# Loading each big weight chunk ahead of the small chunks around it, in the up parts of an expert layer

## The reference, cut to what matters

```python
def _swiglu(h, w_up, w_down):
    g, u = jnp.split(h @ w_up, 2, axis=-1)
    return (jax.nn.silu(g) * u) @ w_down

def _moe(h, w_router, w_up, w_down):
    ...
    top_val, top_idx = lax.top_k(logits, TOP_K)          # 2 of 8 experts for each token
    ...
    for e in range(N_EXPERTS):
        out = out + gates[:, e:e + 1] * _swiglu(hf, w_up[e], w_down[e])
```

## Time and profile before

| what | value |
|---|---|
| three runs | 1743.07, 1746.58, 1746.68 us |
| profiled execution, its time | 1743.41 us |
| its span, first to last instruction | 1741.3 us |
| TensorE busy (PE) | 1638.6 us, 94% |
| VectorE busy (DVE) | 873.3 us, 50% |
| ScalarE busy (ACT) | 652.4 us, 37% |
| moved by DMA | 481.98 MB, mean 277 GB/s |
| loads of expert chunks | 336 of 1 MB: 2 items of 168 |

### The profile page before, as it was taken

How to read it: one execution, slowest core, us unless ns; L and a number is a source line. 1 busy time by engine, 2 the same in 40 slices (tenths; PEclk the granted TensorE clock), 3 DMA queues, 4 the chain that set the end, 5 groups by cost and what they waited for, 6 DMA issues and landing times.

```text
span 1741.3 us, 28335 instructions
## 1 busy us (share of the span) xinstructions
PE 1638.6 (94%) x11532; PEld 1218.1 (70%) x11532; DVE 873.3 (50%) x1305; ACT 652.4 (37%) x956; POOL 28.7 (2%) x49
## 2 busy tenths in 40 slices
PE   5999999999999999999999999998998999899897
PEld 3886568899999777876766667765556666665564
DVE  2434764899997355743763233333433322323447
ACT  2324663544444333424733233333332322323232
POOL 1200000000000000000010000000000000000000
PEclk8999999999999999999999999999999999999999
DMA  9824863133334545333289999999999999999996
GB/s 349 197 97 171 322 233 97 49 98 98 98 122 157 206 146 172 118 97 121 98 297 408 421 421 410 390 401 416 415 422 420 421 421 420 419 416 417 417 417 257
DMA packets 117440, 481.98 MB, mean 277 GB/s; under 512 B 8218, under 2 KB 52424, under 8 KB 68928
## 3 DMA queue, kind: packets, MB, share of 16 engines
q1 hardware_dynamic: 114720, 472.66, 69.2%
q0 software_dynamic: 2592, 7.51, 2.0%
HBM read 477.27 MB, written 2.87 MB: 276 GB/s over the span
## 4 chain that ended last, share of the span: by engine, by line
PE 68%; DMA 13%; DVE 9%; ACT 5%; issue 5%; SPq 0%; DVEq 0%; ACTq 0%
PE PS L1020 17%; PE PS L1022 16%; PE PS L1021 16%; DMA RAWB<-in_w_exp_up 6%; PE PS L1680 4%; DMA RAWB<-in_w_exp_down 3%; PE PS L1052 3%; ACT BH L2346 2%; PE PS L1752 2%; PE PS L1309 2%; DMA RAWA<-in_w_exp_up 2%; DMA RAWA<-in_w_exp_down 1%; PE PS L1319 1%; PE PS L1331 1%; DVE RAWBL L3277 1%
## 5 line engine op out<-in xcount | busy, mean ns | idle before, releaser
L3277 DVE TENSOR_TENSOR RAWBL<-RAWB,BH 128x2048 fp32r<-128x2048 f32 x45 | 103.1, 2292 | 277.2 <-ACT BH L2346 277.2
L1020 PE MATMUL PS<-HH,WH 128*128 128x256 f32 (+1 forms) x600 | 193.5, 323 | 6.3 <-DVE HL L2577 2.9
L1020 PE MATMUL PS<-BH,HE 128*128 128x512 f32 x448 | 182.1, 406 | 12.6 <-DVE RAWBL L3277 11.8
L1022 PE MATMUL PS<-HH,WL 128*128 128x256 f32 (+1 forms) x600 | 190.6, 318 | 0.0
L1021 PE MATMUL PS<-HL,WH 128*128 128x256 f32 (+1 forms) x600 | 190.6, 318 | 0.0
L3277 DVE TENSOR_TENSOR RAWAL<-RAWA,BH 128x2048 fp32r<-128x2048 f32 x39 | 89.4, 2292 | 197.0 <-ACT BH L2346 196.4
L2346 ACT ACTIVATE BH<-RAWB 128x2048 fp32r<-128x2048 f32 x45 | 86.2, 1915 | 239.9 <-DMA RAWB<-in_w_exp_up 120.0
L1022 PE MATMUL PS<-BH,LE 128*128 128x512 f32 x448 | 175.9, 393 | 0.0
L2538 DVE TENSOR_TENSOR WL<-RAW,WH 128x2048 fp32r<-128x2048 f32 (+1 forms) x41 | 91.7, 2237 | 143.0 <-ACT WH L1950 142.7
L2346 ACT ACTIVATE BH<-RAWA 128x2048 fp32r<-128x2048 f32 x39 | 74.6, 1914 | 204.1 <-DMA RAWA<-in_w_exp_up 129.9
L1950 ACT ACTIVATE WH<-RAW 128x2048 fp32r<-128x2048 f32 (+1 forms) x41 | 76.8, 1874 | 141.4 <-PE PS L1022 141.3
(11 more groups left out here) (398 smaller groups left out, 3147.3 us busy)
## 6 DMA issues: line engine op xcount, KB each, us to landing
RAWB<-in_w_exp_up SPq DMA_DIRECT2D x106, 1024.0 KB, 10.5
RAWA<-in_w_exp_up SPq DMA_DIRECT2D x106, 1024.0 KB, 10.6
RAWA<-in_w_exp_down SPq DMA_DIRECT2D x56, 1024.0 KB, 10.0
RAWB<-in_w_exp_down SPq DMA_DIRECT2D x56, 1024.0 KB, 9.8
RAW<-in_w_mod SPq DMA_DIRECT2D x48, 1024.0 KB, 6.8
RAW<-in_w_ffn_up SPq DMA_DIRECT2D x22, 1024.0 KB, 5.5
RAW<-in_w_in_c SPq DMA_DIRECT2D x12, 1024.0 KB, 5.1
RAW<-in_w_ffn_down SPq DMA_DIRECT2D x10, 1024.0 KB, 7.2
```

Source lines behind the costliest of these rows:

```text
L1020: mm(ps, ah, bh, start=start, stop=False)
L1022: return mm(ps, al, bh, start=False, stop=stop)
L3277: v.tensor_tensor(expert_low(big_place(a, i), i), expert_raw(big_place(a, i), i), BH[:, a % 2, :].bitcast(F32), ALU.subtract).then_inc(s_b ...
```

## The change

The list of loads is changed in two places: `up_order`, from which all seven stages of a later item are made, and the last three stages of the first item in `order1`. In a stage of the loop the big chunks stand at places 0, 4, 8 and 12 in place of 2, 6, 10 and 14; in a stage of 12 of the first item they stand at 0, 2, 4 and 8 in place of 1, 3, 6 and 10. With the names from above a stage of the loop is loaded as B s s s B s s s B s s s B s s s, and a stage of 12 as B0 a0 B1 a1 B2 a2 a3 b0 B3 b1 b2 b3. The smalls keep their order among themselves, and so do the bigs.

```diff
-        up_order = [(0, 0), (0, 1), ("big", 0), (0, 2), (0, 3), (1, 0), ("big", 1), (1, 1),
...
+        up_order = [("big", 0), (0, 0), (0, 1), (0, 2), ("big", 1), (0, 3), (1, 0), (1, 1),
...
-            order1 += [(j0, "u", st0, 0), ("big", "u", st, 0), (j0, "u", st0, 1), ("big", "u", st, 1),
...
+            order1 += [("big", "u", st, 0), (j0, "u", st0, 0), ("big", "u", st, 1), (j0, "u", st0, 1),
...
```

More of the change, by code:

```diff
@@ L217, in trunk @@
         NST = EFT // 4
-        up_order = [(0, 0), (0, 1), ("big", 0), (0, 2), (0, 3), (1, 0), ("big", 1), (1, 1),
-                    (1, 2), (1, 3), ("big", 2), (2, 0), (2, 1), (2, 2), ("big", 3), (2, 3)]
+        up_order = [("big", 0), (0, 0), (0, 1), (0, 2), ("big", 1), (0, 3), (1, 0), (1, 1),
+                    ("big", 2), (1, 2), (1, 3), (2, 0), ("big", 3), (2, 1), (2, 2), (2, 3)]
         UPI = NS * NST
@@ L242, in trunk @@
             st = 4 + n
-            order1 += [(j0, "u", st0, 0), ("big", "u", st, 0), (j0, "u", st0, 1), ("big", "u", st, 1),
-                       (j0, "u", st0, 2), (j0, "u", st0, 3), ("big", "u", st, 2), (j1, "u", st1, 0), (j1, "u", st1, 1),
-                       (j1, "u", st1, 2), ("big", "u", st, 3), (j1, "u", st1, 3)]
+            order1 += [("big", "u", st, 0), (j0, "u", st0, 0), ("big", "u", st, 1), (j0, "u", st0, 1),
+                       ("big", "u", st, 2), (j0, "u", st0, 2), (j0, "u", st0, 3), (j1, "u", st1, 0),
+                       ("big", "u", st, 3), (j1, "u", st1, 1), (j1, "u", st1, 2), (j1, "u", st1, 3)]
         assert 1 + 3 * THREES == 4 * 4 and len(PAIRS) - THREES == NST - 4
```

## The result

| | before | after |
|---|---|---|
| runs, median (lowest to highest) | 20 runs: 1745.72 us (1741.98 to 1747.66) | 20 runs: 1749.32 us (1746.71 to 1751.48) |
| ratio | | 1.0027, 95% interval 1.0021 to 1.0033 |
| profiled execution, its span | 1743.41, 1741.3 us | 1749.56, 1747.4 us |

The change makes the kernel slower: by 0.27% or about 4.7 us by the ratio, while the medians lie 3.6 us apart and the means 4.1. The whole interval of the ratio lies just above the 0.2% that the prediction took for the least difference a measurement tells. Of the two profiled executions the one of after is 6.15 us longer. The twenty times of before fall into two groups, 1741.98 to 1745.12 and 1746.33 to 1747.66 us, and the profiled one belongs to the lower, so not all of the 6.15 us is the change's.

A forecast was written before the change was run, and what follows sets the result against it. The prediction took TensorE to bound the kernel from 1040 to 1170 us and the DMA engines afterwards until 1717 us. It added 2.3 us of first-item lag to 1746.58, giving 1748.9 us; 8-in-10 range 1743.5 to 1755.

The forecast's parts named there:

- The first item loses DMA time while TensorE is full: First item, places 76 to 111: waits for big chunks move forward and loads lose 8.7 us, against 5.9 before.
- The lag: 3.0 us at place 114, and at 118 1.5: First two big chunks of the first item's down part: they land 3.0 and 1.5 us later than before.
- the longer step: Between places 114 and 118 before: four chunks took 11.5 us, not 9.9; if repeated, the lag is 3.0, else 1.5.
- I take 2.3: First item's lag at the down part, taken between 1.5 and 3.0 us: 2.3 us added to the time.
- Landing of 5.55 us in a dry queue: First item: a load that finds the DMA queue nearly dry lands 5.55 us after issue; other cases took 7.0 and 7.7.
- In all 8.7 us lost, against 5.9 before: First item: losses of 2.5, 2.5, 1.9 and 1.8 us at places 86, 88, 100 and 112.
- 0.9 us of cover at places 88 and 100: First item: these big chunks are converted 0.9 us or more before TensorE comes to them.
- the upper bound: First item with dry landings of 7.7 us: TensorE 1.2 us late at places 88 and 100, +6 us in all.
- The second item's queue keeps full: Second item's up part: slot reloads have 7.4 or 7.0 us where 5.5 do, so this part costs nothing.
- the rival's mechanism: Second item: reloads leave after the big product and come too late, queue runs dry; 11 us more, 1760, chance 0.13.
- the rival that put 15.3 us on them: TensorE's waits for converted chunks from 1300 to 1600 us were the cost; removing them gives 1731.3 us, chance 0.07.
- The first stall of the second item shrinks: Second item's start: first big product starts about 1308.1, not 1311.4 us; clock may fall less, nothing gained in time.

The follow-up runs named there:

- first_only: Kernel before with the new load order only in the first item's last three stages and the second item's last up stage: 1749.72 us, ratio 1.0036.
- second_only: Kernel before with the new load order only in stages 0 to 5 of the second item: 1745.36 us, ratio 1.0010.
- second_by3: Kernel before with big chunks of the second item's stages 0 to 5 loaded three places earlier: 1764.41 us, ratio 1.0117.
- second_by4: Kernel before with big chunks of the second item's stages 0 to 5 loaded four places earlier: 1901.06 us, ratio 1.0904.
- light_after: Changed kernel with one product in place of three for big chunks in the first item's stages 4 to 6: 1741.10 us, 0.9985 of the kernel before.

## Why the prediction was right in kind and short in size

- *The first item loses DMA time while TensorE is full.* Right, and the loads of 86, 88, 100 and 112 left when B1 and B2 ended, as named; only 88 landed in a dry queue. `first_only` has the cost, and in `second_only` it is within the measurement.
- *The lag: 3.0 us at place 114, and at 118 1.5, or 3.0 if the longer step between landings comes again.* Counted from load 82 the pair of profiles shows 3.0 at 114, 1.5 at 118, and 3.0 from 122 on: the longer step came again, four chunks later.
- *"I take 2.3."* This is the step that failed. It averaged the two, as if the longer step were of that one execution. It should have taken 3.0 at least, and the profiles put 2.9 to 4.2 on the first item (`first_only` and after, loads 75 to 167), the runs 4.7 us by the ratio (3.7 to 5.8 us by its interval). That a landing computed without such steps was set against a recorded one with them made the forecast too small. The time of 1749.32 lies near the forecast of 1748.9 partly by luck: the median of three runs it was added to, 1746.58, is 0.9 above that of twenty. And with 2.3 in the sum the larger chance, 0.58, went to a time that counts as the same; slower, with 0.35, was right.
- *Landing of 5.55 us in a dry queue.* Measured 4.9, 4.8, 7.2 and 4.9. The three rows that it came from say little of a dry queue: each of these loads had 3.0 us of earlier loads still ahead when it left, and the one that took 5.5 us landed 2.5 us behind the load before it, without a gap. The 4.4 us, an estimate from the Trainium skill ("DMA: Bandwidth & Descriptors", Anatomy of one DMA) would have been nearer in three of four cases; the lags worked out from it, 1.9 us at 114 and 0.3 at 118, would have been farther off all the same.
- *In all 8.7 us lost, against 5.9 before.* From load 84 to 114 the landings lose 8.7 and 5.7 us against steps of 2.48, but otherwise spread, so the agreement is partly luck. Of the 2.5, 2.5, 1.9 and 1.8 us put on places 86, 88, 100 and 112, the landings show 0.7, 2.5, 2.8 and none; another 1.3 us are lost at 89, behind the dry queue, and 0.9 at 113.
- *TensorE not late before 1170 us, with 0.9 us of cover at places 88 and 100.* Right at 88; at 100, where the load took 7.2 us, the cover went, as the upper bound had it, and TensorE was later by 0.8 us at the next named issue. The trace after names 0.5 us of it as a wait for the converted chunk, the only one from 1040 to 1170 us:

```profile
PEld PS L1020 <- DVE RAWBL L3277: 0.5, 1, 0.5
```

- *The second item's queue keeps full.* Right: 419 GB/s. It has 27 batches behind a big product, and in the profile all of them left with 4.8 to 5.9 us of loads still to land, without a gap at their own landing. `second_by3` shows the rival's mechanism to be real, one place further on.
- *The waits for converted chunks go, without gain.* Right, against the rival that put 15.3 us on them. From 1300 to 1600 us no wait of L1020 for RAWBL or RAWAL is left among the larger ones; TensorE waits for small chunks in their place:

```profile
PEld PS L1680 <- DMA RAWB<-in_w_exp_up: 19.7, 12, 1.9
...
PE PS L1680 <- DMA RAWB<-in_w_exp_up: 15.4, 13, 1.5
```

- *The first stall of the second item shrinks, and the clock with it.* Right: 6.96 us busy for 2.28 and a granted clock of 1.00 for 0.75, worth nothing in the time. The first copy came at 1308.04 and not about 1304, since the loads were 5.9 us late by then.
- *391 to 394 GB/s from 1040 to 1170 us.* Too high: 383. 17 GB/s over 130 us are 5.3 us of loads, of which some 1.4 arise ahead of the change: the lag is 0.7 us at load 66, which lands as the stretch begins, and 2.1 at load 82.
- *The copy of the down part's first big chunk at 1168 to 1170 us.* It came at 1171.25; of its lag of 5.2 us, 2.1 were there before the change.

## What to carry to other kernels

Where one queue issues loads in order, and each waits for its slot, list them in the order in which the consumer frees the slots: a load moved ahead of that order takes its wait along, and every free slot behind it stands idle. Loading a slowly prepared tile "earlier" in such a ring should pay only if something waits for it on the path that sets the end (argued; no run with the full work gained by it). Here one to two places cost 1 to 2 chunks of transfer where the consumer is the bound, two places nothing clear of noise where the DMA engines are, and three places 15 to 18 us in either part. Compute both sides of a difference with the same model: a smooth replay of the new order against a recorded one of the old hides the steps that the replay leaves out.

## What the runs showed of the hardware

- A 1 MB load of the ring that found no load ahead of it landed 4.7 to 5.0 us after its issue (22 batches in `second_by4`, 4.8 at place 88 in after); with 1.6 and 2.4 us of loads ahead, places 86 and 112 took 4.9 us as well. Back to back, chunks land 2.48 us apart.
- A queue that still holds one chunk can lose time. In `second_by3`, of 18 batches that left with under 4.2 us of loads to land, 16 landed with a gap of 2.7 to 4.9 us in place of 2.48, at their first or second load; with 4.8 us or more left, the first load landed without one in all 27 batches of after, and with 2.7 us once in `second_by3`. Why the queue wants more than the 2.5 us that the plain landing time explains, no run here shows.
- Single steps of 4.0 us between landings also occur with a fuller queue (between places 114 and 122, in both profiles); their cause is open.
- The same big product took 5.74 us at a granted clock of 1.00 and 7.74 us at a mean of 0.72. In `light_after`, where the second stood at the head of SyncE's queue, the lag grew by 3.9 us up to load 200. Of this 3.3 us come by load 184, behind batches that left with 2.3 to 4.1 us of loads to land, and 1.5 at load 193, in a single step of 4.0 us whose cause is open; a long step in the profile of before takes 0.9 off.
